# Four of twenty rounds of value sums taken ahead of the gate stage, sixteen score rows taken behind it

## What is computed

```python
q = (xt @ w_query).reshape(t, PEER_HEADS, 2, PEER_KEY_DIM // 2)
s = jnp.einsum('thpd,hpkd->thpk', q, sub_keys)
s_half, i_half = lax.top_k(s, PEER_TOPK)              # 16 of 128 keys, twice
...                                                    # best 16 of the 16 x 16 pairs
experts, gates = ...                                   # 8 heads x 16 = 128 experts per token
u, vv = expert_u[es], expert_v[es]                     # rows of 16384 x 1024 tables
a = gelu(einsum('tkd,td->tk', u, xs))
y = einsum('tk,tkd->td', gs * a, vv)
```

## Time and profile before

| | us |
|---|---|
| median of 3 runs | 1979.25 |
| lowest, highest | 1977.19, 1988.70 |
| the profiled execution, its time | 1982.75 |
| the profiled execution, its span (first to last instruction) | 1980.9 |

### The profile page before, as it was taken

The page is one execution under the profiler, slowest core; times in us unless marked ns, Lnnn a source line. Parts: engine busy times, 40 slices in busy tenths (PEclk is TensorE's granted clock), DMA queues, the critical chain, the costliest instruction groups (busy, mean ns, idle before and its releaser), DMA issues.

```text
span 1980.9 us, 21746 instructions
## 1 busy us (share of the span) xinstructions
PE 1838.6 (93%) x8148; PEld 1190.8 (60%) x8148; DVE 1292.5 (65%) x2583; ACT 285.1 (14%) x660; POOL 892.1 (45%) x837
## 2 busy tenths in 40 slices
PE   5888999999999999998999999997779989999995
PEld 2676744467544348997888888885544434434442
DVE  1111476689668758999998876668865623326767
ACT  0120010046400001111111110006530000000000
POOL 1010136567545512325455554666765655435440
PEclk8998999989999999999999999999999999999997
DMA  8894939888899878649999999998889989999995
GB/s 355 367 360 187 361 139 359 301 304 311 291 379 338 325 276 306 206 176 364 361 366 368 387 388 408 409 392 300 293 311 410 409 351 409 409 409 409 409 410 220
DMA packets 166713, 670.23 MB, mean 338 GB/s; under 512 B 19370, under 2 KB 19498, under 8 KB 160972
## 3 DMA queue, kind: packets, MB, share of 16 engines
q0 software_dynamic: 112512, 410.79, 55.3%
q1 hardware_dynamic: 49344, 242.24, 31.1%
q10 hardware_dynamic: 4752, 15.81, 2.1%
HBM read 659.27 MB, written 7.39 MB: 337 GB/s over the span
## 4 chain that ended last, share of the span: by engine, by line
PE 65%; DMA 18%; DVE 8%; POOL 5%; issue 3%; ACT 1%; ACTq 0%; DVEq 0%; POOLq 0%
PE psum L788 22%; DMA arena<-in_expert_v_dram,arena 9%; PE psum L663 7%; PE psum L935 7%; PE psum L851 6%; POOL arena L516 5%; PE psum L900 4%; DMA arena<-in_expert_u_dram,arena 4%; PE psum L865 3%; PE psum L868 3%; DVE arena L1344 3%; PE psum L816 2%; DMA arena<-in_w_ada_dram 2%; PE psum L877 1%; PE psum L875 1%
## 5 line engine op out<-in xcount | busy, mean ns | idle before, releaser
L516 POOL DMA_INDIRECT arena<-in_expert_u_dram,arena x384 | 469.9, 1224 | 365.5 <-DVE arena L1344 241.9
L1344 DVE CUSTOM_DVE_ANT_0 arena<-arena 128x1024 f32<-128x1024 f32 x384 | 461.9, 1226 | 200.2 <-DMA arena<-in_expert_u_dram,arena 198.9
L516 POOL DMA_INDIRECT arena<-in_expert_v_dram,arena x384 | 379.5, 988 | 416.9 <-DVE psum L1578 221.7
L1578 DVE SCALAR_TENSOR_TENSOR psum<-arena,psum 128x1024 f32<-128x1024 f32 x254 | 327.1, 1288 | 204.2 <-DMA arena<-in_expert_v_dram,arena 192.5
L788 PE MATMUL psum<-arena 128*128 128x256 f32 x2048 | 445.4, 380 | 6.3 <-DMA arena<-in_expert_uT_dram 6.3
L851 PE MATMUL psum<-arena 128*128 128x512 f32 x1024 | 444.0, 595 | 1.4 <-DMA arena<-in_expert_v_dram 1.4
L788 PEld LDWEIGHTS psum<-arena 128*128 128x128 f32 x2048 | 390.4, 191 | 60.1 <-issue 6.6
L851 PEld LDWEIGHTS psum<-arena 128*128 128x128 f32 x1024 | 194.0, 190 | 252.7 <-issue 252.7
L935 PE MATMUL psum<-arena 128*128 128x128 f32 x1280 | 146.2, 275 | 0.4 <-DVE arena L1492 0.4
L935 PEld LDWEIGHTS psum<-arena 128*128 128x128 f32 x1280 | 144.4, 192 | 1.5 <-issue 0.9
L663 PE MATMUL psum<-arena 128*128 128x512 f32 x320 | 137.7, 592 | 0.0
(11 more groups left out here) (174 smaller groups left out, 1418.9 us busy)
## 6 DMA issues: line engine op xcount, KB each, us to landing
arena<-in_expert_uT_dram SPq DMA_DIRECT2D x128, 512.0 KB, 6.8
arena<-in_expert_v_dram SPq DMA_DIRECT2D x128, 512.0 KB, 6.8
arena<-in_w_in_dram SPq DMA_DIRECT2D x16, 2048.0 KB, 10.0
arena<-in_w_ada_dram SPq DMA_DIRECT2D x12, 2048.0 KB, 15.0
arena<-in_w_query_dram SPq DMA_DIRECT2D x8, 2048.0 KB, 14.4
arena<-in_w_in_dram SPq DMA_DIRECT2D x16, 512.0 KB, 7.0
arena<-in_w_o_dram SPq DMA_DIRECT2D x4, 2048.0 KB, 13.6
arena<-in_expert_u_dram,arena POOLq DMA_INDIRECT x384, 9.2
```

What stands on the lines that cost most here:

```text
L516: pool.indirect_dma_start(slots[b], None, table[0], bass.IndirectOffsetOnAxis(ap=numbers[:, b - b0:b - b0 + 1], axis=0)).then_inc(lands[b] ...
L1344: dve.tensor_tensor_reduce(UR[b], UR[b], U2B[e], 1.0, 0.0, ALU.mult, ALU.add, DOTS[e % 2][:, k:k + 1]).then_inc(u_free, 1)
L1578: dve.scalar_tensor_tensor(ys, row, weight, ys, ALU.mult, ALU.add).then_inc(v_free, 1)
```

## The change

Four rounds of tile 1's value sums leave the gate stage. They stand on TensorE behind the score blocks 54, 57, 60 and 63. The gate stage keeps 16 rounds, one behind every second batch. The score rows of tile 2 that stand ahead of the rounds on GpSimd and VectorE are 56 (7 groups) in place of 72, and those behind the gate stage 72 in place of 56. The number of rounds ahead of the value blocks stays 20, and the table `ROUND_AFTER` stays as it is. No instruction is added or taken away.

```diff
@@ -955,10 +955,12 @@
                 if m == WEIGHTS_AT:
                     rank_weights()
                 expert_scores(m)
+                if m in SCORE_ROUND_AFTER:
+                    sum_round(SCORE_ROUND_AFTER[m])
             for i in range(BATCHES):
                 place(i)
-                for r in range(i * GATE_ROUNDS // BATCHES, (i + 1) * GATE_ROUNDS // BATCHES):
-                    sum_round(r)
+                if i % 2 == 1:
+                    sum_round(SCORE_ROUNDS + i // 2)
             for n in range(NKEYS):
                 expert_values(n)
                 if n in ROUND_AFTER:
@@ -1707,7 +1709,9 @@
-SCORED_GROUPS, GATE_ROUNDS = 9, 20
+SCORED_GROUPS, SCORE_ROUNDS = 7, 4
+GATE_ROUNDS = SCORE_ROUNDS + BATCHES // 2
+SCORE_ROUND_AFTER = {54 + 3 * r: r for r in range(SCORE_ROUNDS)}
```

## The result

The changed kernel takes 2024.24 us (median of 4 runs, 2019.88 to 2029.11) and the kernel before 1981.2 us in the same comparison: a ratio of 1.0218, 95% interval 1.0199 to 1.0236. It is slower by 43 us; 33.6 us were forecast, and the value lies inside the range, 11 us over the point of 2012.9. Run once more beside the last experiments, it gave 2025.53 us against 1981.15, a ratio of 1.0225 (1.0195 to 1.0255).

A forecast was written before the change was run, and what follows sets the result against it. The prediction took two resources as near their end, TensorE (busy 93%) and the transfers (350 to 410 GB/s). Terms: 24 + 6.1 + 2.0 - 20.5 + 22 = +33.6 us, giving 2012.9 us, range 2000 to 2025.

The forecast's parts named there:

- wait behind block 54: Score blocks: TensorE reaches the first sum before its gathered rows and stands 24 us, bounds 19 and 34.
- restart at the lower clock: Score blocks, after the wait: TensorE starts at its lower clock, costing 2.0 us (1.4 to 2.7).
- four sums: Score blocks: three sums cost 5.6 us, the fourth, ahead of the first placing, 0.5; together 6.1 us.
- gate stage: With 16 rounds VectorE sets the pace; of its 22.4 us of waiting 2 us stay, gain 20.5 us.
- value blocks to round 20: Ahead of round 20: 16 more gathers with nothing to cover them cost 22 us, bounds 20.5 and 32.5.
- behind it: Value blocks after round 20: order and bytes as before, no change in time.
- the round's own 3.7 and 6.5 us: Wait behind block 54: first round's gathers need 3.7 us to issue and 6.5 us to land.
- by-bytes estimate: Wait behind block 54: 7.8 loads of the stopped stream at 409 GB/s save 10 of 34 us, leaving 24.
- loop of the buffers: Gate stage: a buffer set returns after 10.5 us plus 1.9 us for the sum, 12.4 us.
- No wait: Rival, score blocks: no wait at the first sum, total +7.6 us, 1987 us; chance 5%.
- Only bytes count: Rival, whole program: transfers are the bound, the stop costs nothing, not slower, 1979 us; chance 3%.
- The gathers don't speed up: Rival, score and value blocks: gathers stay as slow when the stream stops, +54.1 us, 2033 us; chance 9%.

The follow-up runs named there:

- Experiments 1 and 2: 1: changed kernel with its four sums behind score blocks 60 to 63, ratio 1.0080. 2: changed kernel with 40 score rows ahead, 88 behind, ratio 1.0167.
- Experiment 4: Kernel before with 16 rounds in the gate stage in place of 20, the other four behind it, no sum in the score blocks: 1986.01 us, ratio 1.0044.
- experiment 5: Against the changed kernel: 64 score rows ahead, two sums behind score blocks 62 and 63, 18 rounds in the gate stage: 1983.56 us, ratio 1.0017.
- Experiment 3: Kernel before with 56 score rows ahead of the rounds and 72 behind, nothing else moved: 2003.8 us, ratio 1.0125.
- experiment 6: Late rounds put behind later value blocks in three kernels, two run again; changed kernel with sums behind blocks 60 to 63: 1985.02 us, ratio 1.0021.
- e1: Changed kernel with its four early sums behind score blocks 60, 61, 62 and 63: 1995.53 us, ratio 1.0080.
- e2: Kernel before with 16 rounds in the gate stage and 16 behind it, no sum in the score blocks: 1986.01 us, ratio 1.0044.
- e7: Changed kernel with sums behind score blocks 60 to 63, rounds 20 and 21 behind value blocks 44 and 46: 1993.79 us, ratio 0.9908, second chip.
- e8: Kernel before with 16 rounds in the gate stage, 16 behind it from value block 37 on: 1982.01 us, ratio 0.9849, second chip.
- f3: Changed kernel with sums behind score blocks 60 to 63, rounds 20 and 21 behind value blocks 44 and 46, third chip: 1985.02 us, ratio 1.0021.
- e6: Kernel before with rounds 20 and 21 behind value blocks 37 and 39, the others from 43 on: 2000.87 us, ratio 0.9939, second chip.
- e5: Changed kernel with 40 score rows ahead of the rounds and 88 behind: 2047.12 us, ratio 1.0167, second chip.

## Why the prediction was right, and where it was off

Term by term, from the two profiled executions (their spans differ by 43.2 us):

| term | forecast | measured |
|---|---|---|
| wait behind block 54 | 24 | 29.3 |
| restart at the lower clock | 2.0 | 2.6 (3.64 for 1.92, at a granted clock of 0.50; 21.90 for 20.99) |
| four sums | 6.1 | 5.6 in the score stage, the fourth inside the gate stage |
| gate stage | -20.5 | -20.9 |
| value blocks to round 20 | +22 | +24.6 |
| behind it | 0 | +1.8 |

The mechanism was right in each stage. The misses don't cancel one another: nearly all make the kernel slower than forecast, and only the width of the range holds them.

- **The order decides.** TensorE reached the first sum 29 us before its rows, as read from two clocks of the old trace: the end of block 54 and the row that frees the buffer. Experiments 1 and 2 take the wait away from either side, by moving the sum and by moving the fetch. This is shown.
- **The size of the wait was the mis-sized term.** The step that failed was "the round's own 3.7 and 6.5 us": the four gathers needed 6.04 us to issue where 3.7 were counted. The landing was nearly right (6.06 us from the fourth issue at 1298.39 to the sum). The rest is small: the gathers started at 1292.35 and not at 1290.3, because row 52 ended 0.9 us later than counted (1291.24) and GpSimd was then busy for 1.1 us with the group before; TensorE arrived 0.55 us sooner (1275.15); and 24 us were taken where this chain gave 24.8. Together that is the 29.3 us. The by-bytes estimate, which agreed with the other, was right in the bytes and wrong in the rate: 24 us at 409 GB/s are 9.8 MB, and the wait moved 9.9 MB at 339 GB/s.
- **The gate stage came as worked out**, from VectorE's 3.6 us per batch (115 us for 32). Experiment 4 shows it for 16 rounds with nothing changed ahead of the stage. The loop of the buffers, 12.4 us, doesn't by itself give the times with 20 and 18 rounds, 13.9 and 13.5 us for a pair (experiment 5); with 14.4 us to hide in, that did no harm.
- **The value blocks** cost 24.6 us where 22 were taken; the bounds were 20.5 and 32.5. It is all in round 20's wait (32.51 less 7.87), in which the transfers ran at 336 GB/s and not at 409; 8.39 MB at 336 GB/s are an estimated 25 us. Experiment 3 shows the same 24.6 us with the rows moved and nothing else. The forecast's reason, that nothing covers them, holds; experiment 6 adds that moving the rounds gives back some 10 us only, those in which the transfers weren't full.
- **The rivals.** "No wait" is what e1 shows for another place of the sums: 1.0080 and 1.0069 in the two comparisons against the forecast 7.6 us (1.004), since the value blocks up to round 20 cost 2.6 us more and the last stretch is about 1 us longer; the remaining 3 to 5 us aren't attributed. "Only bytes count" falls for the score stage and holds for the larger part, 16 of 26 us, behind the gate stage. "The gathers don't speed up" falls: from row 44 (1278.53) to row 52 (1290.01) VectorE took 1.44 us per row in place of 2.03, without a wait between the last six.
- **What came out ahead.** f4 (16 rounds in the gate stage, none in the score blocks, rounds behind from block 37 on) is faster than the kernel before by 0.24%, with an interval of 0.08 to 0.40%. Of the gate stage's 21 us, the 16 gathers and four sums that stand behind it take 25.8 back in e2 and 14.2 in f4 (518.8 us for 504.6).

**What stays open.** Why the kernel before took 2012 us on the second chip, where no trace of it was kept, and why e7 and e8 rose by only 9 and 6 us there (against f3 and f4). e6 was not run elsewhere, so whether the kernel before gains by moving round 20 alone isn't settled.

## What to carry to other kernels

Before moving work up in an engine's program, read two times from the old trace: when the engine will reach it, and when the buffer that its data needs is freed in the order of the queue that fetches it. Room in one stage is worth only what the stages that take the work instead have to spare: count the full transfers and the busy matmuls there first. Where bytes set the end, a gap in front of an instruction costs only what the transfers leave out in it: read their rate inside the gap, or move the gap once and see how much comes back.

## What the runs showed of the hardware

**A gather takes longer to issue beside some of VectorE's instructions, not when many are under way.** GpSimd's instruction takes 0.94 us in most cases and up to 1.97 us in the wait of the changed kernel (the rows above), which adds 2.3 us to a round of four. Counted over the whole trace of the changed kernel, 172 of its 768 gathers take more than 1.05 us. 146 of them overlap one of VectorE's score instructions (which read two operands in the arena, the core's on-chip memory), of 294 gathers that do. Of the 226 that overlap a value row (one operand in the arena, one in PSUM) three are long, and of the 127 that overlap no instruction of VectorE none. The number under way doesn't show in it: in the 35 us of e6 below all 22 gathers take 0.93 or 0.94 us, though 12.97 MB of gathers pass in them. This is counted from traces; no run takes VectorE's rows away from beside the gathers.

**On one chip, loads of the stream were issued late beside many gathers.** In e6 TensorE stood twice near the end, 11.29 and 16.09 us, with the transfers full. SyncE's loads in this time, then the transfer view of 1815 to 1850 us, then that of 1846 to 1852 us (queue, packets, MB, share):

```profile
1801.88 0.33 SPq L478 DMA_DIRECT2D arena<-in_expert_v_dram  x1
1820.02 0.33 SPq L478 DMA_DIRECT2D arena<-in_expert_v_dram  x1
1842.47 0.33 SPq L478 DMA_DIRECT2D arena<-in_expert_v_dram  x1
```

```profile
q0 software_dynamic: 3563, 12.97, 92.9%
q1 hardware_dynamic: 367, 1.37, 9.8%
...
q1 hardware_dynamic: 332, 1.23, 51.3%
q0 software_dynamic: 331, 1.21, 50.6%
```

In 35 us GpSimd's queue moved 12.97 MB and the queue of the stream 1.37, less than three of its pieces, while TensorE waited for the next one. The loads were issued late: ordinarily one follows another after 3.4 us, here after 18.1 and 22.5 us, though TensorE had used up all four buffers by 1815.6 us. Once issued, a load is served as fast as ever (1820.02 to 1826.87, 1842.47 to 1849.26, where TensorE goes on). The Trainium skill (DMA: Bandwidth & Descriptors, Queues, rings and completion order) says that each engine goes round its queues packet by packet. The trace agrees where both queues have requests: 332 and 331 packets from 1846 to 1852 us. By the program only a freed buffer holds a load in the value blocks; the profile puts 41.9 us of SyncE's waits down to "remote", and what that was stays open. By then the rounds are through and the value rows of tile 2 are fetched into 16 buffers in place of eight. e5 has the same two gaps (12.59 and 16.02 us) behind loads that are 19.6 and 21.7 us apart, e7 has three of 2.7 to 3.6 us and e8 one of 2.1; all four ran on the second chip, and no kernel on the other chips shows such a gap.
